# Four of each feed-forward's eleven steps as two pairs of seven block products, with the sums of the token blocks ahead of each feed-forward's first pair on VectorE

## The reference, cut to what matters

```python
def _swiglu(x, w1, w3, w2):
    return (jax.nn.silu(x @ w1) * (x @ w3)) @ w2      # w1, w3: 1024 x 2816, w2: 2816 x 1024
# first block, per layer: layernorm(ALPHA * x + 0.5 * swiglu(x)), a mixer, the same again
# second block, per layer: x + 0.5 * rms_norm(swiglu(rms_norm(x, g0)), g1), a mixer, the same again
```

## Time and profile before

| | |
|---|---|
| median of 3 runs | 2430.61 us |
| the profiled execution: its time, its span | 2428.91 us, 2427.1 us |
| PE busy | 2384.7 us, 98% of the span |
| DVE busy | 1455.4 us, 60% |
| ACT busy | 1070.6 us, 44% |
| POOL busy | 119.6 us, 5% |
| mean granted TensorE clock | 0.997 |
| read from HBM | 422.49 MB, 175 GB/s over the span |

### The profile page before, as it was taken

The page is one execution under the profiler, slowest core; times in us unless marked ns, Lnnn a source line. Parts: engine busy times, 40 slices in busy tenths (PEclk is TensorE's granted clock), DMA queues, the critical chain, the costliest instruction groups (busy, mean ns, idle before and its releaser), DMA issues.

```text
span 2427.1 us, 29857 instructions
## 1 busy us (share of the span) xinstructions
PE 2384.7 (98%) x11668; PEld 1974.2 (81%) x11668; DVE 1455.4 (60%) x1599; ACT 1070.6 (44%) x1308; POOL 119.6 (5%) x145
## 2 busy tenths in 40 slices
PE   9999999999999999999999999999999999999998
PEld 8888887888888888788887887798888888787887
DVE  5456866654654656775556456797545545656544
ACT  4443355344344343644344434534434434555442
POOL 0001000000000000000001002102000000110000
PEclk9999999999999999999999999999999999999999
DMA  8565534655655555355574566303556556344552
GB/s 279 187 218 197 190 110 159 206 190 190 207 173 185 195 200 194 123 207 174 185 239 141 190 220 208 93 1 124 193 188 206 182 183 225 107 156 147 183 190 87
DMA packets 281236, 426.58 MB, mean 176 GB/s; under 512 B 11747, under 2 KB 193635, under 8 KB 281136
## 3 DMA queue, kind: packets, MB, share of 16 engines
q1 hardware_dynamic: 273632, 400.04, 49.5%
q0 software_dynamic: 7520, 25.37, 3.4%
HBM read 422.49 MB, written 1.05 MB: 175 GB/s over the span
## 4 chain that ended last, share of the span: by engine, by line
PE 83%; DVE 12%; ACT 2%; issue 1%; POOL 1%; DMA 0%; DVEq 0%; POOLq 0%; SPq 0%; ACTq 0%
PE bank L1909 25%; PE bank L1911 25%; PE bank L1910 24%; DVE wl L1120 4%; PE bank L2366 2%; PE bank L2056 1%; PE bank L1956 1%; POOL rstd L463 1%; DVE stats L1155 1%; DVE arena L1618 1%; DVE y L1222 1%; DVE x L1164 1%; PE bank L2159 1%; DVE y L1189 1%; DVE x L1225 1%
## 5 line engine op out<-in xcount | busy, mean ns | idle before, releaser
L1120 DVE TENSOR_TENSOR wl<-wf,wh 128x2048 fp32r<-128x2048 f32 x355 | 808.4, 2289 | 420.7 <-ACT wh L622 420.2
L1909 PE MATMUL bank<-wh,xTh 128*128 128x512 f32 x2336 | 925.7, 396 | 13.8 <-DVE wl L1120 7.5
L1911 PE MATMUL bank<-wh,xTl 128*128 128x512 f32 x2336 | 910.0, 390 | 0.0
L1910 PE MATMUL bank<-wl,xTh 128*128 128x512 f32 x2336 | 908.7, 389 | 0.0
L622 ACT ACTIVATE wh<-wf 128x2048 fp32r<-128x2048 f32 x355 | 673.3, 1915 | 244.5 <-PE bank L1911 237.2
L1909 PEld LDWEIGHTS bank<-wh,xTh 128*128 128x128 f32 x2336 | 439.1, 188 | 105.8 <-issue 7.6
L1911 PEld LDWEIGHTS bank<-wh,xTl 128*128 128x128 f32 x2336 | 438.9, 188 | 93.2
L1910 PEld LDWEIGHTS bank<-wl,xTh 128*128 128x128 f32 x2336 | 439.6, 188 | 86.5 <-issue 0.7
L1909 PE MATMUL bank<-wh,hTh 128*128 128x512 f32 x704 | 277.2, 394 | 0.2
L1911 PE MATMUL bank<-wh,hTl 128*128 128x512 f32 x704 | 274.9, 391 | 0.0
L1910 PE MATMUL bank<-wl,hTh 128*128 128x512 f32 x704 | 274.5, 390 | 0.0
(11 more groups left out here) (333 smaller groups left out, 1500.5 us busy)
## 6 DMA issues: line engine op xcount, KB each, us to landing
wf<-in_ffn_w SPq DMA_DIRECT2D x160, 512.0 KB, 4.8
wf<-in_w_in SPq DMA_DIRECT2D x52, 1024.0 KB, 5.5
wf<-in_ffn_w SPq DMA_DIRECT2D x44, 1024.0 KB, 5.0
wf<-in_ffn_w_down SPq DMA_DIRECT2D x44, 1024.0 KB, 5.0
wf<-in_ffn_w_gate SPq DMA_DIRECT2D x80, 512.0 KB, 4.0
wf<-in_ffn_w_up SPq DMA_DIRECT2D x80, 512.0 KB, 4.9
wf<-in_w_branch SPq DMA_DIRECT2D x16, 1024.0 KB, 5.1
wf<-in_c_w_in SPq DMA_DIRECT2D x14, 1024.0 KB, 5.9
```

What stands on the lines that cost most here:

```text
L1120: dve.tensor_tensor(wl[s], wf[s], wh[s].bitcast(f32), ALU.subtract).then_inc(SEM[f"lo{s}"], 1)
L1909: pe.matmul(o, lh, rh, start=start, stop=False)
L1910: pe.matmul(o, lh, rl, start=False, stop=False)
L1911: return pe.matmul(o, ll, rh, start=False, stop=stop)
```

## The change: what it does

Steps 2 to 9 of each feed-forward are now written out as two bodies of four steps, ja, jb, jc and jd. Steps ja and jb are computed as before. Steps jc and jd are computed as a pair: the token matrix is cut into four blocks A11, A12, A21, A22 (128 tokens by 512), the two steps' weights into four units B11, B21 (step jc), B12, B22 (step jd), and the four blocks of the product C come from seven block products for eight. A block product is 12 matmuls of 512 columns.

- `block_sums` (DVE, once per feed-forward, at the head of the first body) makes four combinations of token blocks by ten operations of 128 x 512; they are kept in slot 5 and split like a weight unit (`cast(5)`, `low(5)`).
- In each body DVE makes four combinations of weight units, 128 x 2048 each: B12 - B11 into `wf0`, B22 - B12 into `wf1`, their combination T = B22 - B12 + B11 into `wf4`, and B21 - T into `wf2`. Three of the seven operands are units as loaded, four are such combinations, so there are seven casts and seven rests for the pair where there were four.
- ACT copies a partial sum out of PSUM three times (`snapshot`, 128 x 512), DVE adds it to another bank three times (`block_of`, 128 x 512); Silu and gating then run on the four blocks of C, 256 columns each, in `y` (`c_silu`, `c_gated`), and their eight transposes go to `bank6` and `bank7` (`blocks_hidden`).
- Slots are used in another order, and SP's loads are reordered to fit. The load of jb's w2 goes to slot 4 and additionally waits for the rest of T (`lo3`), since T lies in `wf4` until then.
- The loops are gone on all engines; some semaphores of the mixers are merged.

The core of the diff (left out: the same renumbering of slots in the heads, semaphore names, counters):

```diff
--- before.py
+++ after.py
+BODIES = (STEPS - 3) // 4
...
+    yq = [y[:, i // 2, (i % 2) * HALF:(i % 2 + 1) * HALF] for i in range(4)]
+    C11, C21, C12, C22 = yq
+    part_v, part_1, part_5 = C21, C12, C22
+    sumA = wf[5].rearrange("p (j k t) -> p j k t", j=4, k=4)
+    sumA_h, sumA_l = (t[5].rearrange("p (j k t) -> p j k t", j=4, k=4) for t in (wh, wl))
+    SUM1, SUM2, SUM3, SUM4 = range(4)
+    bankX, bankY, bankZ = (bank[i][:, :] for i in (4, 5, 7))
...
+            c.count("lo5")
+            for i in range(BODIES):
+                ja, jb, jc, jd = range(2 + 4 * i, 6 + 4 * i)
+                if i == 0:
+                    up_unit(w1, w3, ja, 3, 0)
+                    up_unit(w1, w3, ja, 4, 1)
+                    down(w2, 1)
+                up_unit(w1, w3, jb, 3, 0)
+                up_unit(w1, w3, jb, 1, 1)
+                down(w2, ja, 0)
+                up_unit(w1, w3, jc, 4, 0)
+                up_unit(w1, w3, jd, 1, 0, "b12_ld")
+                up_unit(w1, w3, jd, 3, 1, "b22_ld")
+                up_unit(w1, w3, jc, 2, 1)
+                sp.wait_ge(SEM["lo3"], c.so_far("lo3"))
+                down(w2, jb, 4)
+                for n in ("lo0", "lo2", "lo3"):
+                    c.count(n)
+                up(w1, w3, jd + 1, 0)
+                down(w2, jc, 4 if i < BODIES - 1 else 5)
+                sp.wait_ge(SEM["lo3"], c.so_far("lo3"))
+                down(w2, jd, 2)
             down(w2, STEPS - 1, 3)
-            with c.loop(STEPS - 2, "sp ffn") as j:
-                up(w1, w3, j + 2, 0)
-                down(w2, j + 1)
...
+        def cast(s, src):
+            act.wait_ge(SEM[f"used{s}"], c.so_far(f"used{s}"))
+            c.count(f"used{s}")
+            act.activation(wh[s], src, ACT.Copy).then_inc(SEM[f"hi{s}"], 1)
+
+        def snapshot(to, s):
+            act.wait_ge(SEM[f"used{s}"], c.so_far(f"used{s}"))
+            act.activation(to, bankX, ACT.Copy).then_inc(SEM["snap"], 1)
+
+        def c_silu(to, src):
+            act.activation(to[:, 0:STEP], src[:, 0:STEP], ACT.Silu).then_inc(SEM["h_silu"], 1)
+
...
+            for i in range(BODIES):
+                if i == 0:
+                    prep(1, 2)
+                    prep(0)
+                    prep(3, 2)
+                    act.wait_ge(SEM["t_made"], c.next("t_made"))
+                    cast(5, wf[5])
+                    act.wait_ge(SEM["used4"], c.so_far("used4"))
+                    silus()
+                else:
+                    prep(3, 2)
+                    take_both(1)
+                    take_both(0, 7)
+                    prep(0)
+                    act.wait_ge(SEM["used1"], c.so_far("used1"))
+                    silus()
+                    prep(1, 2)
+                prep(4, 2)
+                take_both(1)
+                prep(2, 2)
+                act.wait_ge(SEM["t_made"], c.next("t_made", 3))
+                cast(3, wf[4])
+                act.wait_ge(SEM["used1"], c.so_far("used1"))
+                silus()
+                cast(1, wf[1])
+                cast(0, wf[0])
+                take_both(0)
+                snapshot(part_1, 4)
+                prep(4)
+                act.wait_ge(SEM["c_made"], c.next("c_made"))
+                c_silu(C11, C11)
+                act.wait_ge(SEM["b22_ld"], c.next("b22_ld", 32))
+                cast(2, wf[3])
+                snapshot(part_v, 3)
+                act.wait_ge(SEM["t_made"], c.next("t_made"))
+                cast(3, wf[2])
+                snapshot(part_5, 0)
+                prep(0, 2)
+                act.wait_ge(SEM["c_made"], c.next("c_made"))
+                c_silu(C22, C22)
+                prep(1, 2)
+                if i < BODIES - 1:
+                    prep(4)
+                act.wait_ge(SEM["used2"], c.so_far("used2"))
+                c_silu(C12, bankX)
+                if i < BODIES - 1:
+                    prep(2)
+                else:
+                    prep(5)
+                act.wait_ge(SEM["c_made"], c.next("c_made"))
+                c_silu(C21, C21)
+            prep(2)
+            take_both(1)
+            take_both(0, 7)
...
+        def low_of(s, src):
+            dve.wait_ge(SEM[f"hi{s}"], c.next(f"hi{s}"))
+            c.count(f"used{s}")
+            c.count(f"lo{s}")
+            dve.tensor_tensor(wl[s], src, wh[s].bitcast(f32), ALU.subtract).then_inc(SEM[f"lo{s}"], 1)
...
+        def block_sums():
+
+            def A(b, r, t):
+                return t[:, 4 * r:4 * r + 4, b * P:(b + 1) * P].bitcast(f32)
+
+            s1, s2, s3, s4 = (sumA[:, j, :, :] for j in range(4))
+            dve.tensor_tensor(s1, A(1, 0, xTh), A(1, 1, xTh), ALU.add)
+            dve.tensor_tensor(s2, A(1, 0, xTl), A(1, 1, xTl), ALU.add)
+            dve.tensor_tensor(s3, A(0, 0, xTh), A(1, 0, xTh), ALU.subtract)
+            settle(dve.tensor_tensor(s4, A(0, 0, xTl), A(1, 0, xTl), ALU.subtract))
+            dve.tensor_tensor(s1, s1, s2, ALU.add)
+            settle(dve.tensor_tensor(s3, s3, s4, ALU.add))
+            settle(dve.tensor_tensor(s2, s1, A(0, 0, xTh), ALU.subtract))
+            settle(dve.tensor_tensor(s2, s2, A(0, 0, xTl), ALU.subtract))
+            settle(dve.tensor_tensor(s4, A(0, 1, xTh), s2, ALU.subtract))
+            dve.tensor_tensor(s4, s4, A(0, 1, xTl), ALU.add).then_inc(SEM["t_made"], 1)
+            c.count("t_made")
+
+        def block_of(to, part, bk):
+            dve.tensor_tensor(to, part, bk, ALU.add).then_inc(SEM["c_made"], 1)
+
+        def c_gated(to, up, half):
+            dve.wait_ge(SEM["h_silu"], c.next("h_silu"))
+            dve.scalar_tensor_tensor(to[:, 0:STEP], to[:, 0:STEP], half, up[:, STEP:2 * STEP], ALU.mult, ALU.mult)\
+               .then_inc(SEM["h_ready"], 1)
...
+            for i in range(BODIES):
+                if i == 0:
+                    block_sums()
+                    low(3)
+                    both_gated(half)
+                    low(1)
+                    low(0)
+                else:
+                    low(3)
+                    take_both(1)
+                    take_both(0, 7)
+                    low(0)
+                    both_gated(half)
+                    low(1)
+                low(4)
+                dve.wait_ge(SEM["b12_ld"], c.next("b12_ld", 32))
+                dve.wait_ge(SEM["lo0"], c.so_far("lo0"))
+                dve.tensor_tensor(wf[0], wf[1], wf[4], ALU.subtract).then_inc(SEM["t_made"], 1)
+                dve.wait_ge(SEM["b22_ld"], c.next("b22_ld", 32))
+                dve.tensor_tensor(wf[1], wf[3], wf[1], ALU.subtract).then_inc(SEM["t_made"], 1)
+                take_both(1)
+                if i == 0:
+                    low(5)
+                dve.wait_ge(SEM["t_made"], c.next("t_made", 2))
+                dve.tensor_tensor(wf[4], wf[1], wf[4], ALU.add).then_inc(SEM["t_made"], 1)
+                low(2)
+                both_gated(half)
+                dve.wait_ge(SEM["t_made"], c.next("t_made"))
+                dve.tensor_tensor(wf[2], wf[2], wf[4], ALU.subtract).then_inc(SEM["t_made"], 1)
+                low_of(3, wf[4])
+                low_of(1, wf[1])
+                low_of(0, wf[0])
+                take_both(0)
+                dve.wait_ge(SEM["t_made"], c.next("t_made"))
+                dve.wait_ge(SEM["snap"], c.next("snap"))
+                dve.wait_ge(SEM["used2"], c.so_far("used2"))
+                block_of(C11, part_1, bankY)
+                low(4)
+                c_gated(C11, C11, half)
+                low_of(2, wf[3])
+                low_of(3, wf[2])
+                dve.wait_ge(SEM["snap"], c.next("snap", 2))
+                block_of(C22, part_5, bankZ)
+                low(0)
+                c_gated(C22, C22, half)
+                low(1)
+                if i < BODIES - 1:
+                    low(4)
+                c_gated(C12, bankX, half)
+                dve.wait_ge(SEM["used3"], c.so_far("used3"))
+                block_of(C21, part_v, bankZ)
+                c_gated(C21, C21, half)
+                if i < BODIES - 1:
+                    low(2)
+            low(5)
+            take_both(1)
+            take_both(0, 7)
+            low(2)
             low(3)
-            with c.loop(STEPS - 3, "dve ffn"):
-                low(0)
-                for b in range(TB):
-                    ins = gated(b, 4 + b, half)
-                ins.then_inc(SEM["h_ready"], 1)
-                low(1)
-                dve.wait_ge(SEM["ht_hi"], c.next("ht_hi"))
-                dve.tensor_tensor(hTl[0][:, :, :], bank[6][:, :].rearrange("p (k t) -> p k t", k=2),
-                                  hTh[0][:, :, :].bitcast(f32), ALU.subtract).then_inc(SEM["ht_ready"], 1)
-                low(2)
...
+        def product(s, lhs, o, start, freed=None):
+            pe.wait_ge(SEM[f"lo{s}"], c.next(f"lo{s}"))
+            for q, (lh, ll) in enumerate(lhs):
+                r = slice(q * HALF, (q + 1) * HALF)
```

(51 more changed lines are left out.)

## The result

The changed kernel takes 2460.36 us (median of 4 runs, 2459.13 to 2462.44), the kernel before 2430.6 beside it: ratio 1.0126, 95% interval 1.0114 to 1.0138. It is slower, by 30 us. The forecast was 2446 with a range up to 2460. The sign and the places were right; of the 30 us it had 15.

What follows compares the result with a forecast made beforehand. PE was taken as the bound, busy 2384.7 of 2427.1 us; 54.7 us of new waits against 43.5 saved took 2428.9 to 2440.1, 5 us of clock to 2445, and 1.7 to the runs' median gave 2446, range 2416 to 2460.

Steps and rivals of the forecast that it cites:

- The saving: Up matmuls on PE: twelve fewer per pair of steps at 0.2267 us, 16 pairs, 43.5 us saved.
- The places: First bodies: PE waits 0.4 us at ja's transposes, 2.1 at its `down`, 2.0 at jb's transposes, 2.6 at fifth product.
- The chain: First bodies: DVE, a load and ACT reach the fifth product at +51.6 us, PE without a wait at +44.5.
- walk: DVE's queue followed through a first body from PE's first product after the head: 7.1 us of waits per feed-forward.
- the 0.4 us that the walk allowed for a late cast: Low pass of slot 3, after the sums: 0.4 us allowed for its cast, so it starts at +13.9.
- The clock: Granted clock falling behind first-body waits: 8 x 0.75 x 0.5 x 1.7 = 5 us.
- the fourth: Wait of PE at the fifth block product of a first body for ACT's snapshot, 2.6 us.
- The rule that only a fall behind the last wait is paid: First bodies: clock loss behind the second or third wait mostly comes out of the next; behind the fourth it is paid.
- The half: Chance of a half that the clock falls behind a wait of about 2 us, from two of four waits.
- the forecast without clock: Whole program: 54.7 us of new waits against 43.5 saved, +11.2, giving 2440.1 us.
- The clock falls every time: Rival: each feed-forward pays 1.7 us behind its fourth wait, 2440 + 8 x 1.7 = 2454 us; chance 0.12.
- the sums open the chain: Head of each first body: the ten block sums on DVE, 6.55 us, stand before everything else and end at +13.5.

Runs made afterwards that it cites:

- e8: Changed kernel with slots 1 and 0 loaded before slot 3, sums in the head, `hTl` before the B12/B22 waits, snapshot before the cast of jb's w2: 2404.13 us.
- e9: Changed kernel plus 9 filler matmuls of 128 columns before the fifth block product of each first body: 2452.34 us.
- e10: Changed kernel plus fillers in first bodies: 8 before the `down` of the step before ja, 6 before the transposes of jb: 2457.12 us.
- e2: Changed kernel with nine of the ten token block sums left out, so three combined products are not the reference's: 2456.59 us.
- e7: Changed kernel with slots 1 and 0 loaded before slot 3 in first bodies, and sums in the head's idle time except in the first feed-forward: 2429.02 us.
- e1: Changed kernel plus filler matmuls at three places of each first body, the fillers of e10 and those of e9 together: 2448.65 us.

## Why the prediction was right in kind and wrong in size

The mechanism came as forecast; two terms of the sum were too small, the clock behind the last wait most of all, then the chain.

- *The saving.* 43.5 us forecast; 39.4 us of PE's work went in the changed kernel, 41.7 in e8. The 192 matmuls are exact. What is missing goes with the waits: a matmul is listed at 0.39 us but costs 0.2267, so behind every wait some 0.16 us of busy time is not overlapped. That reading fits roughly (28 more waits than before by 0.16 are 4.5 us where 4.1 are missing, in e8 16 by 0.16 are 2.6 where 1.8 are missing) but no run tested it.
- *The places.* Waits at the `down` of ja, the transposes and the fifth product of each first body and none in the second bodies: right. The `down` has 16.9 us and the fifth product 20.3, where 8 times 2.1 and 2.6 were forecast. The transposes have 11.1, where 8 times 2.4 were: in five feed-forwards the clock fell behind the `down`, and these 8.5 us are taken out of the wait at the transposes of jb.
- *The chain.* Mis-sized by 1.2 us a feed-forward. From PE's first product behind the head, mean of the last seven:

  | | walk | measured |
  |---|---|---|
  | low pass of slot 3 starts | +13.9 | +14.4 |
  | B12 - B11 starts | +24.4 | +25.2 |
  | B22 - B12 starts | +27.4 | +28.4 |
  | the cast of jb's w2 starts | +47.1 | +48.3 |
  | fifth product | +51.7 | +52.9 |

  Half a microsecond stands at the first link: the 0.4 us that the walk allowed for a late cast was 0.2 to 0.3 in four feed-forwards and 1.5 in three. The rest is in the loads, 0.2 to 0.3 at each of three; w2 took 5.2 us in the mean, not 5.0. 7 x 1.2 = 8.3 us, and 0.3 in the first feed-forward.
- *The clock.* The step that failed is "with a chance of a half at each, the fourth is long enough in some three of four cases: 8 x 0.75 x 0.5 x 1.7 = 5 us". The term measured 13.6 us. Part of it is the length: all eight of these waits were long enough (2.07 to 3.65 us), not six. The other part is the chance: the clock fell behind 7 of the 8, behind one of them for 3.4 us. The rule that only a fall behind the last wait is paid held, as e9 and e10 show. The half was read from four waits, and the trace had a fifth of nearly that length, with a fall behind it, so three of five:

```profile
1565.55 1.76 PE L2366 MATMUL bank<-wf 128*128 128x128 f32 x11 [1.87 <-DVE wf L1605]
```
```profile
1567.00:1568.00 1.00, 1.00 (x7) 1.00 (x7) 0.54 (x1) 0.00 (x0) 0.00 (x0) 0.50 0.00 0
```

  Of all 20 waits of 1.8 us and more in the changed kernel 15 have a fall behind them, of its shorter ones none. At the fifth product of the other variants it is 21 of 41, so a half was no bad guess for such a wait; that the changed kernel got 7 of 8 no row of before could tell.
- *The sum.* 2440.1 (the forecast without clock) + 8.3 + 0.3 + 13.6 = 2462.3. The profiled execution took 2462.44. That it closes to 0.1 us is in part chance: outside of the first bodies the clock lost 8.9 us against 7.0 before, which the sum leaves out.
- *The rivals.* "The clock falls every time" (2454) had the right mechanism; with the chain's 8.6 us it is the result. It had a chance of 0.12, too little. The Trainium skill ("TensorE: Matmul & The Clock Gate", section "What's actually happening") has the throttled rate as the default that activity releases. By that rule the clock should rather fall behind such waits: the trace of the changed kernel agrees in 7 of 8, those of the variants in 21 of 41.
- *A step right by luck.* The walk has the sums open the chain and allows 0.4 us for a cast that is late. e2 shows that this cast alone would have held the low pass just as long. The number nearly stood; the edit built on it, e2, gained 4 us where its expectation had 45 to 65 under this theory.

## What to carry to other kernels

Where a chain through other engines sets the end of a stretch, list all that its first link waits for before naming one of them as the cause; taking one away shows nothing while another of the same length stands beside it. A wait of 2 us that comes last in such a chain costs its own length and with it, at times, the clock behind it (1.7 us, in 7 of 8 places in the changed kernel and 21 of 41 in its variants), while an earlier one is mostly given back; so cut the last link first, or fill it with matmuls that do nothing. And a scheme that takes work from the bounding engine needs its new operations placed in the idle time of the engine that makes them: the same seven products cost 30 us in one order and gain 26 in another.

## What the runs showed of the hardware

- Runs of one and the same kernel differ with their mean granted clock: e7's go from 2422.53 us at 0.994 to 2431.92 at 0.991. A fall can be twice as long as the others (at 545.88 in the changed kernel it misses 3.4 us of full rate, not 1.7).
- A wait as long at the same place is not always followed by a fall: behind the fifth product 7 of 8 in the changed kernel, 2 of 8 in e10, with waits of 20.3 and 20.4 us in all.
- Matmuls added to a waiting PE shortened the program: e1 has 184 more (368 rows of the trace) than the changed kernel and takes 11.7 us less.
